# Six more block pairs with seven products: the second down projection of a two-block fp32 layer on Trainium2

## The reference, cut to what matters

```python
def conv_glu(hn, w_up, conv_w, conv_b, w_down):
    up = hn @ w_up
    gate, val = jnp.split(up, 2, axis=-1)
    gate = dwconv_centred(gate, conv_w, conv_b)
    return (jax.nn.gelu(gate, approximate=True) * val) @ w_down
...
        hn = rmsnorm(h, ffn_norm_pre[i])
        ff = conv_glu(hn, w_ffn_up[i], ffn_conv_w[i], ffn_conv_b[i], w_ffn_down[i])
        h = h + rmsnorm(ff, ffn_norm_post[i])
        gate = jax.nn.sigmoid(rmsnorm(h, ple_norm_pre[i]) @ w_ple_gate[i])
        h = h + rmsnorm(gate * (p[i] @ w_ple[i]), ple_norm_post[i])
```

## Time and profile before

| | |
|---|---|
| median of 3 runs | 2374.06 us (2373.86 to 2374.58) |
| the profiled execution | 2373.92 us |
| its span | 2372.1 us |
| TensorE busy | 2357.3 us (99%), 11866 instructions |
| VectorE busy | 1580.5 us (67%) |
| ScalarE busy | 1205.8 us (51%) |
| GpSimd busy | 342.9 us (14%) |
| DMA | 444.02 MB, 187 GB/s on average |

### The profile page before, as it was taken

How to read it: one execution, slowest core, us unless ns; L and a number is a source line. 1 busy time by engine, 2 the same in 40 slices (tenths; PEclk the granted TensorE clock), 3 DMA queues, 4 the chain that set the end, 5 groups by cost and what they waited for, 6 DMA issues and landing times.

```text
span 2372.1 us, 29924 instructions
## 1 busy us (share of the span) xinstructions
PE 2357.3 (99%) x11866; PEld 1978.7 (83%) x11866; DVE 1580.5 (67%) x2001; ACT 1205.8 (51%) x1627; POOL 342.9 (14%) x302
## 2 busy tenths in 40 slices
PE   9999999999999999999999999999999999999999
PEld 7878898888888888888788888887888888888887
DVE  7898578779876775575765556657565554656556
ACT  7866455445544444465655555535444444444442
POOL 1262016326412221000000000001000000000000
PEclk9999999999999999999999999999999999999999
DMA  8445655665666656665666565565666666666653
GB/s 297 155 147 196 213 181 184 199 187 180 211 201 189 190 188 210 195 199 173 180 183 206 152 203 160 169 187 168 190 181 180 216 188 198 178 183 179 189 178 125
DMA packets 122939, 444.02 MB, mean 187 GB/s; under 512 B 13744, under 2 KB 15408, under 8 KB 122288
## 3 DMA queue, kind: packets, MB, share of 16 engines
q1 hardware_dynamic: 122800, 442.12, 60.1%
HBM read 439.97 MB, written 2.10 MB: 186 GB/s over the span
## 4 chain that ended last, share of the span: by engine, by line
PE 93%; DVE 4%; ACT 2%; DMA 1%; issue 1%; SPq 0%; DVEq 0%; ACTq 0%
PE bank L822 92%; DVE wlo L1709 1%; DMA raw<-in_w 1%; DVE ev L1712 1%; ACT whi L1237 1%; PE bank L971 0%; DVE hT L1712 0%; DMA hT<-in_xT 0%; DVE hn L1712 0%; PE bank L1223 0%; PE bank L1156 0%; ACT hT L1405 0%; PE bank L1178 0%; DVE xa L1712 0%; ACT L1411 0%
## 5 line engine op out<-in xcount | busy, mean ns | idle before, releaser
L1709 DVE TENSOR_TENSOR wlo<-raw,whi 128x1024 fp32r<-128x1024 f32 (+2 forms) x811 | 1029.0, 1275 | 703.3 <-ACT whi L1237 700.9
L1237 ACT ACTIVATE whi<-raw 128x1024 fp32r<-128x1024 f32 (+2 forms) x813 | 849.3, 1050 | 908.0 <-PE bank L822 869.9
L822 PE MATMUL bank<-xa,whi 128*128 128x512 f32 (+1 forms) x2688 | 841.9, 395 | 6.8 <-DVE xa L1712 3.3
L822 PE MATMUL bank<-whi,xa 128*128 128x512 f32 x2048 | 639.4, 393 | 2.2 <-DVE wlo L1709 1.8
L822 PEld LDWEIGHTS bank<-xa,wlo 128*128 128x128 f32 x2656 | 497.6, 188 | 115.1
L822 PE MATMUL bank<-xa,wlo 128*128 128x256 f32 (+1 forms) x2656 | 521.1, 278 | 0.0
L822 PE MATMUL bank<-whi,xb 128*128 128x512 f32 x1456 | 449.3, 390 | 0.0
L822 PEld LDWEIGHTS bank<-whi,xa 128*128 128x128 f32 x2048 | 379.7, 188 | 82.6 <-issue 4.7
L822 PEld LDWEIGHTS bank<-xa,whi 128*128 128x128 f32 x2688 | 411.2, 188 | 16.0 <-issue 6.6
L822 PE MATMUL bank<-wlo,xa 128*128 128x512 f32 x1024 | 399.1, 390 | 0.0
L822 PEld LDWEIGHTS bank<-whi,xb 128*128 128x128 f32 x1456 | 272.3, 188 | 56.6 <-DVE wlo L1709 0.3
(11 more groups left out here) (269 smaller groups left out, 1455.9 us busy)
## 6 DMA issues: line engine op xcount, KB each, us to landing
raw<-in_w SPq DMA_DIRECT2D x803, 512.0 KB, 3.7
hT<-in_ln_rows SPq DMA_DIRECT2D x2, 2048.0 KB, 8.6
raw<-in_w SPq DMA_DIRECT2D x9, 256.0 KB, 2.7
X<-in_post SPq DMA_DIRECT2D x3, 768.0 KB, 5.4
S<-in_x SPq DMA_DIRECT2D x4, 512.0 KB, 7.4
hT<-in_x SPq DMA_DIRECT2D x1, 2048.0 KB, 8.2
out<-S SPq DMA_DIRECT2D x8, 256.0 KB, 2.5
hT<-in_xT SPq DMA_DIRECT2D x3, 512.0 KB, 7.7
```

What stands on the lines that cost most here:

```text
L822: return pe.matmul(o, w, x, start=start, stop=stop, skip_group_check=True)
L1237: act.activation(hi, r, ACT.Copy).then_inc(*w_high(i))
L1709: return dve.tensor_tensor(o, x, y, op)
```

## The change

Down projection 1 is computed through `paired_out` as well. In its left half the k-pairs 0 and 1 (of its eleven) take seven products, behind six plain turns; in its right half the k-pairs 0 to 3, with two plain turns in each but the last, which has none. It has 56 turns.

- The mixtures of k-pairs 0 and 1 are made during up projection 1 (`EARLY[1]`, which was there already), those of 2 and 3 behind the left half's pairs, on the turns of `MIXES`, in memory of `xa`, which is free then.
- Column 0 and column 2 of this projection are evacuated 5 turns behind the half's last pair (2 in down projection 0).
- The gain row is loaded at turn -50 from the end, not -40, into `wide` (the memory of `xa`), no longer into `X` and `ev`; the squares of this projection write to `wide` too.

```diff
-PLANS = ((plan((0, 1, 2, 3), 2, (2, 2, 2, 2)), plan((0, 1, 2, 3), 2, (2, 2, 2, 2))), (plan((0, 1), 6, (2, 2)), plan((0, 1, 2, 3), 1, (2, 2, 2, 0))))
-IN_PAIRS = (0,)
+PLANS = ((plan((0, 1, 2, 3), 2, (2, 2, 2, 2)), plan((0, 1, 2, 3), 2, (2, 2, 2, 2))), (plan((0, 1), 6, (2, 2)), plan((0, 1, 2, 3), 2, (2, 2, 2, 0))))
+IN_PAIRS = (0, 1)
+MIXES = ((2, 3, 7, 8), (3, 9, 12, 13))
...
-            late(d + 2, kind, pair[0])
-            for after, p in mixes if c == 0 else ():
-                mix(d + after, 1, p)
+            late(d + (5 if k else 2), kind, pair[0])
+            for p, *after in mixes if c == 0 else ():
+                mix(d, 1, p, *after)
...
-    def mix(u, half, p):
-        late(u, "mixed", half, p)
-        late(u + 2, "mixed_high", half, p)
-        late(u + 3, "mixed_low", half, p)
+    def mix(u, half, p, sums=0, high=2, low=3):
+        late(u + sums, "mixed", half, p)
+        late(u + high, "mixed_high", half, p)
+        late(u + low, "mixed_low", half, p)
...
-    late(d - 40, "load_post", 1)
+    late(d - 50, "load_post", 1)
...
+        def post_row(r, c):
+            if r == 1:
+                return wide[:, 4096 + 512 * c:4608 + 512 * c]
...
+                        if r == 1:
+                            q.wait_ge(*piece_tile.of("used", XA_FREE[1]))
+                            for i in range(2):
+                                sp.dma_start(wide[:, 4096 + 1024 * i:5120 + 1024 * i],
+                                             a["post"][1:2, 1024 * i:1024 * i + 1024].broadcast_to((128, 1024))).then_inc(post_in, 16)
+                            continue
...
-                act.activation(scratch[len(squared) % 3], x, ACT.Square, accum_out=total).then_inc(*squares(*name))
+                into = wide[:, 2048 + 512 * (len(squared) % 3):2560 + 512 * (len(squared) % 3)] if name[:2] == ("ss", 1) else scratch[len(squared) % 3]
+                act.activation(into, x, ACT.Square, accum_out=total).then_inc(*squares(*name))
```

More of the change, by code:

```diff
@@ L316, in layout @@
         if half in IN_PAIRS:
-            ends["down", half] = paired_out(f"down{half}", ("ff",), "w_ffn_down", 22 * half, *PLANS[half], mixes=((7, 2), (13, 3)) if half else ())
+            ends["down", half] = paired_out(f"down{half}", ("ff",), "w_ffn_down", 22 * half, *PLANS[half], mixes=MIXES if half else ())
         else:
@@ L641, in block_kernel @@
                   ((0, 0), (0, 1), (0, 2), (1, 0), (1, 1), (0, 3), (1, 2), (1, 3)))
-        def post_row(c):
+        def post_row(r, c):
+            if r == 1:
+                return wide[:, 4096 + 512 * c:4608 + 512 * c]
             return X[:, 512 * c:512 * c + 512] if c < 3 else flat(ev[:, 0:2, :])
@@ L786, in sync_program @@
                         else:
-                            q.wait_ge(*(vec_val.of("weighted", 1, 1, 3) if r == 2 else vec_evac.of("tile", tile_of["mix", 3] + 1)))
+                            q.wait_ge(*vec_val.of("weighted", 1, 1, 3))
                             q.wait_ge(*x_low.of("p", 1))
-                            if r == 1 and 0 in IN_PAIRS:
-                                q.wait_ge(*piece_tile.of("used", LAST_SUMS))
                         sp.dma_start(X[:, 0:1536], a["post"][r:r + 1, 0:1536].broadcast_to((128, 1536))).then_inc(post_in, 16)
-                        sp.dma_start(post_row(3), a["post"][r:r + 1, 1536:D].broadcast_to((128, 512))).then_inc(post_in, 16)
+                        sp.dma_start(post_row(r, 3), a["post"][r:r + 1, 1536:D].broadcast_to((128, 512))).then_inc(post_in, 16)
                     elif step == "load_p":
@@ L1812, in weigh @@
                 q.wait_ge(post_in, 32 * r + 32)
-                return tt(sn[:, t, 512 * c:512 * c + 512], x, post_row(c), ALU.mult)
+                return tt(sn[:, t, 512 * c:512 * c + 512], x, post_row(r, c), ALU.mult)
             def rms_sum(r, t):
```

## The result

The changed kernel takes 2380.9 us (median of 7 runs, 2379.82 to 2381.58) against 2374.06 (7 runs): a ratio of 1.0027, 95% interval 1.0017 to 1.0037. It is 6.8 us slower, where I had forecast 1.6 and allowed 2379.0 at most.

The account below looks back on a forecast made before the run. TensorE, busy 99% of the span, was taken as the bound. Products saved, waits in the right half and waits behind the projection gave -4.1 + 0 + 5.9 = +1.8 on 2373.92: 2375.7 us, range 2370.2 to 2379.0.

Parts of the forecast that it names:

- The product and the saving: Second down projection on TensorE: each product costs 0.68 us; six pairs drop one each, 18 matmuls, saving 4.1 us.
- Early mixtures, gain row, squares, left half's splits: Added preparation work on GpSimd, ScalarE and VectorE, and the gain row's load, would cost TensorE zero.
- The right half's last pair: End of the right half's pairs: the last full sums' split arrives in time, 0 us of waiting, bounds 0 and 3.4.
- my second rival: Right half: GpSimd starts the second pair's sums late, delaying the last full sums by 3.4 us; 2379.1 us, chance 0.12.
- The tail: Behind the last seven-product pair: column 3 comes 6.6 us late, 0.7 of it hidden, so TensorE waits 5.9 us.
- (a): Behind the last pair: ScalarE's copy of the first side bank comes at T + 6.9.
- T: The moment TensorE ends the last seven-product pair of the second down projection, with six plain turns remaining, to T + 16.3.
- (b): Behind the side bank's copy: VectorE's folding is done 5.0 us later, at T + 11.9.
- (c): Behind the fold: GpSimd's four additions to the first half's sums, 5.2 to 7.8 us, taken as 6.5, to T + 18.4.
- (d): Behind the additions: VectorE's column 2 and the next split take 4.3 us, so column 3 starts at T + 22.7.
- Tail hidden: Behind the last pair: weights land in time, column 3 is 1.4 late, 0.7 felt; 2370.5 us, chance 0.26.
- The engines exclude each other: GpSimd's additions and VectorE's splits behind the fold run in turn, 8.9 us instead of 6.5; 2378.1 us, chance 0.08.

Follow-up runs that it names:

- the run with the mixtures moved: The changed kernel with the mixtures of k-pairs 2 and 3 made before the left half's four GpSimd additions instead of after them; 2379.54 us.
- additions by column: The changed kernel with GpSimd doing column 2's two right-half additions before column 3's, and VectorE's column 2 finish waiting only for those; 2377.78 us.
- two places for the sums: The changed kernel with every other right-half pair's sums in a second place, so they need not wait for the previous pair's split; 2379.17 us.

## Why the prediction was wrong

- **The product and the saving** (0.68 us, 4.1 in all): right but for small steps. 18 matmuls left. But a projection with pairs takes 0.5 to 0.8 us more than 0.68 for each product, spread over steps of 0.02 or so, even where TensorE never waits. The earlier trace rows had it: 168 products in 114.78 us, where 168 x 0.68 = 114.2. I put it at nothing.
- **Early mixtures, gain row, squares, left half's splits** (zero): right. TensorE has no new wait ahead of 985.
- **The right half's last pair** (zero, bounds 0 to 3.4): **this is the step that failed.** It rested on the second pair's sums starting 6.8 us behind the left half. TensorE's right half starts at 967.68 in the trace; the sums start at 976.89, **9.2** behind. The surplus of 2.4 us lands on the end as the text said of each us beyond 6.8: waits that add 1.8 us at the last full sums and 0.5 at the second pair's. Another 0.8 is spread in small steps, which the run without late mixtures has too (0.7). Together 3.1. The waits are my second rival, in mechanism. That rival gave GpSimd 34.7 us from the left pairs' end (942.9) to the second pair's sums; it took 34.0. Its price was 3.4, against 2.3 of waits. I gave it 0.12 although my own sum found "nothing to spare", and argued against it by one duration, the mixture's. The second fault was to let VectorE open the loop at 31.3. It is there at 976.60, 33.7: its column finishes and splits run beside a GpSimd without a pause. The run with the mixtures moved shows that this second limit alone keeps 0.8 of the 2.3 us of waits.
- **The tail** (+5.9, measured 7.4): the order of its steps was right, their sizes in part not. (a) The copy came at T + 6.4 against 6.9, and with it (b) the fold at T + 11.4 against 11.9. (c) The additions took 7.86 us, not 6.5, just outside my bounds of 5.2 to 7.8. I had taken a middle pace between "alone" and "beside splits"; there is no pace, but an order of turns (next point). Then 0.45 us to column 2, at T + 19.8. (d) 4.2 us to column 3: T + 24.0 against 22.7. With 0.7 hidden, 24.0 - 16.1 - 0.7 = 7.2, measured 7.4. That TensorE's recorded wait is 4.2 and not 7.4 is in the main the clock's doing, below.
- **Tail hidden** (2370.5) did not happen with four pairs, but its condition, room behind the last pair, is what the versions with two and three pairs meet, at 2371.8 and 2371.0.
- **The engines exclude each other** (2378.1, chance 0.08): its mechanism is what the trace shows. I had argued against it from merged rows; asked for one by one, the same instructions stand like this, GpSimd and then VectorE in the changed kernel's tail:

```profile
1022.78 2.21 POOL L2423 TENSOR_TENSOR S<-S,wide 128x512 f32<-128x512 f32 x1 [15.38 <-DVE wide L1717]
...
1024.95 2.26 POOL L2423 TENSOR_TENSOR S<-S,wide 128x512 f32<-128x512 f32 x1
...
1027.17 2.24 POOL L2423 TENSOR_TENSOR S<-S,wide 128x512 f32<-128x512 f32 x1
...
1029.38 1.26 POOL L2423 TENSOR_TENSOR S<-S,wide 128x512 f32<-128x512 f32 x1
```

```profile
1022.61 1.22 DVE L1717 TENSOR_TENSOR wlo<-raw,whi 128x1024 fp32r<-128x1024 f32 x1
...
1023.75 2.32 DVE L1717 TENSOR_TENSOR wlo<-raw,whi 128x1024 fp32r<-128x1024 f32 x1
...
1025.99 2.30 DVE L1717 TENSOR_TENSOR wlo<-raw,whi 128x1024 fp32r<-128x1024 f32 x1
```

  The ends alternate: 1023.83, 1024.99, 1026.07, 1027.21, 1028.29, 1029.41, 1030.64, each 1.1 to 1.2 us behind the last. A duration of 2.2 to 2.3 holds the time for which the instruction was blocked. Seven instructions one after the other take 8.03 us from 1022.61, 1.15 each; my 8.9 took 1.24 and 1.29 for them, which hold some 0.1 of overlap at the ends. By this, step (c) is four additions and three splits in turn, which no middle pace describes. The Trainium skill (SBUF — State Buffer, "Who interferes with whom") states that a VectorE operation with two SBUF inputs contends with a GpSimd operation that reads SBUF, and that the port pair they share is an exclusive lock. The trace agrees, with the ends above.

  Why I read it otherwise: in the earlier trace rows I set 8.4 us against a serial 10.1. One of the four splits there is half as large, which its merged row hides:

```profile
634.84 1.78 DVE L1709 TENSOR_TENSOR wlo<-raw,whi 128x512 fp32r<-128x512 f32 x1
```

  and with the 1.15 of the change's tail it is 3.5 x 1.15 + 4 x 1.15 = 8.6; from 633.71 to the last sum's end at 642.26 the trace has 8.55. No overlap. The same turns fit the run with the mixtures moved: their GpSimd operations block VectorE wherever they stand, and that is argued, not shown by a run of its own.
- **No effect**: out.
- Both losses at once, 3.1 and 7.4, were the case that my range left out: the rival of the loop kept the tail at 5.9 and came to 2379.1. With the tail's measured 7.4 it gives 2380.6. That this is so near the measured time is partly luck: its 3.4 for the loop is too much for the waits and leaves out the small steps.

## What to carry to other kernels

When a saving on the bounding engine is paid for by work on engines that feed it, give each saved unit its slack: here three pairs fit in front of eight plain turns, and with the fourth, worth 0.68 us, the kernel was 9.9 slower. A step for which the sum leaves nothing to spare is to be priced as a loss, and work that GpSimd does in SBUF beside two-input VectorE operations is to be added to VectorE's time, row by row and not from merged rows. And when several results are handed over by one signal, ask which of them the first reader needs: putting two additions ahead of the other two was worth 3.1 us.

## What the runs showed of the hardware

- **Which VectorE operations block GpSimd.** In the stretches looked at, only those with two SBUF inputs did. In the run with the additions by column, column 2's two evacuations (one input in PSUM) start at 1027.97, beside the third addition, and take their usual 1.27 us together:

```profile
1026.93 2.25 POOL L2424 TENSOR_TENSOR S<-S,wide 128x512 f32<-128x512 f32 x1
```

  The addition is let go at 1028.05 by the last split and ends at 1029.18, 1.13 later, as in the sequence above. In the change, the addition at 958.18 takes 1.29 us beside column 0's evacuations. The three splits ahead of them take 5.68 us beside the additions, and 3.49 where there are none. VectorE's busy time on the page, 43.8 us more than before for 24 more instructions, is therefore partly time in which it was blocked.
- **The granted clock after a short wait.** Windows of the changed kernel:

```profile
1025.00:1030.00 5.00, 2.78 (x13) 1.96 (x11) 3.29 (x2) 0.00 (x0) 5.00 (x3) 0.99 0.74 212
1030.00:1035.00 5.00, 3.07 (x7) 2.48 (x8) 3.47 (x5) 3.17 (x6) 0.63 (x1) 0.50 0.30 104
1035.00:1040.00 5.00, 5.00 (x21) 3.97 (x20) 4.49 (x11) 3.79 (x11) 0.00 (x0) 0.82 0.38 105
```

  In the window in which the wait of 4.15 us ends, the granted clock was 0.50, the 1.2 GHz level, and four products, from 1031.93 to 1037.00, took 5.1 us instead of 2.7. The two runs that also had a single wait of over 4 us (mixtures moved, two places for the sums) show clocks of 0.61 and 0.66 in that window; the runs whose waits there were up to 1.8 us stayed at 1.00. Here it cost little: the slow products fill time in which TensorE would have waited for the growth of `h` anyway. That is worked out from the rows: the first transpose comes 1.0 us behind the growth's first operation, against 0.8 in the runs with six pairs and no drop, and in the run with two places, whose clock is back at 1.00 from 1035 on. In the run with the mixtures moved five products are slow (1031.88 to 1038.20), and the distance is 1.6. (That run's profile is also 1.3 us late at the projection's start, behind a clock of 0.66 from 180 to 185 us, which has nothing to do with the edit.) So a wait on paper is not TensorE's whole loss, and its busy time not its work.
